# Starting the stages behind a row norm with one row tile at a time, in an eight-stage transformer kernel

## What is computed

```
x = first_block(x, ...)                       # ends: x + rms_norm(mixed @ w_o) * g
for layer in (0, 1):
    y = gla_mixer(x) if layer == 0 else moba_mixer(x)     # both end in @ w_out
    x = layer_norm_2(ALPHA * x + y, ln_g[layer, 0], ln_b[layer, 0])
    gate, up = split(x @ w_gu)                            # 1024 x 5632
    x = layer_norm_2(ALPHA * x + (silu(gate) * up) @ w_down, ln_g[layer, 1], ln_b[layer, 1])
# gla: q, k, v, g, gk_low = split(x @ w_in), chunked gated linear attention
# moba: q, k, v = split(x @ w_in), 8 heads of 128, q and k rotated (32 of 128 dims), softmax attention
```

## Time and profile before

| | |
|---|---|
| median of 3 runs | 929.03 us (928.59 to 933.44) |
| the profiled execution | 928.22 us |
| its span from first to last instruction | 926.5 us |
| PE busy | 888.3 us, 96% |
| DVE busy | 608.5 us, 66% |
| ACT busy | 438.6 us, 47% |
| POOL busy | 121.2 us, 13% |
| mean granted clock of PE | 0.986 |

### The profile page before, as it was taken

One profiled execution on the slowest core, in us unless ns is written; L12 is line 12 of the kernel. 1 busy time (PEld: TensorE's weight loads), 2 busy tenths in 40 slices (PEclk: granted clock), 3 DMA queues, 4 the chain that ended last, 5 costly groups with the idle time before them and its releaser, 6 DMA issues.

```text
span 926.5 us, 14261 instructions
## 1 busy us (share of the span) xinstructions
PE 888.3 (96%) x6011; PEld 813.1 (88%) x6011; DVE 608.5 (66%) x861; ACT 438.6 (47%) x606; POOL 121.2 (13%) x109
## 2 busy tenths in 40 slices
PE   6999989999999999989999999989999899999994
PEld 5997989998888888779999988779988899999883
DVE  5996995777567755784555544676887755555446
ACT  5555453555645853434444443334574444444330
POOL 0433430121002101020000000023600100000002
PEclk9999999999999999999999999989999999999998
DMA  8663665663347552546666555446634565655541
GB/s 300 190 181 91 190 189 143 175 170 112 104 127 237 170 162 81 167 144 189 187 186 182 183 186 192 151 153 195 192 114 141 172 187 184 183 182 185 192 146 46
DMA packets 117801, 154.20 MB, mean 166 GB/s; under 512 B 5263, under 2 KB 95786, under 8 KB 117706
## 3 DMA queue, kind: packets, MB, share of 16 engines
q1 hardware_dynamic: 116266, 148.31, 52.5%
q0 software_dynamic: 1472, 4.98, 1.7%
HBM read 151.44 MB, written 1.05 MB: 165 GB/s over the span
## 4 chain that ended last, share of the span: by engine, by line
PE 85%; DVE 12%; DMA 1%; issue 1%; ACT 1%; DVEq 0%; SPq 0%
PE acc L527 25%; PE acc L528 24%; PE acc L529 24%; PE acc L565 3%; DVE w_lo L1471 2%; DVE conv L1618 2%; DVE y L1902 1%; DVE rs L1504 1%; PE misc L653 1%; DVE stats L1889 1%; PE misc L717 1%; DVE y L1877 1%; DVE rs L1508 1%; DVE sc_acc L1638 1%; PE misc L898 1%
## 5 line engine op out<-in xcount | busy, mean ns | idle before, releaser
L1471 DVE TENSOR_TENSOR w_lo<-staged,w_hi 128x1024 fp32r<-128x1024 f32 x274 | 339.6, 1249 | 224.7 <-ACT w_hi L1073 224.2
L1073 ACT CAST w_hi<-staged 128x1024 fp32r<-128x1024 f32 x274 | 285.0, 1045 | 238.3 <-DMA staged<-in_ffn_w_gu 69.1
L527 PE MATMUL acc<-x_hi,w_hi 128*128 128x256 f32 (+1 forms) x1296 | 367.6, 284 | 3.1 <-DVE m L1697 3.1
L528 PE MATMUL acc<-x_lo,w_hi 128*128 128x256 f32 (+1 forms) x1296 | 366.9, 283 | 0.0
L529 PE MATMUL acc<-x_hi,w_lo 128*128 128x256 f32 (+1 forms) x1296 | 364.1, 281 | 0.0
L527 PEld LDWEIGHTS acc<-x_hi,w_hi 128*128 128x128 f32 x1296 | 243.7, 188 | 5.5 <-DVE m L1697 3.3
L529 PEld LDWEIGHTS acc<-x_hi,w_lo 128*128 128x128 f32 x1296 | 246.0, 190 | 0.0
L528 PEld LDWEIGHTS acc<-x_lo,w_hi 128*128 128x128 f32 x1296 | 244.4, 189 | 0.4 <-issue 0.2
L2258 POOL TENSOR_TENSOR y<-y,gain 128x512 f32<-128x512 f32 x8 | 10.7, 1338 | 460.1 <-ACT y L1269 460.1
L529 PE MATMUL acc<-w_hi,h_lo 128*128 128x512 f32 x176 | 69.6, 396 | 0.0
L527 PE MATMUL acc<-w_hi,h_hi 128*128 128x512 f32 x176 | 69.6, 395 | 0.0
(11 more groups left out here) (369 smaller groups left out, 1124.2 us busy)
## 6 DMA issues: line engine op xcount, KB each, us to landing
staged<-in_ffn_w_gu SPq DMA_DIRECT2D x88, 512.0 KB, 3.5
staged<-in_w_in SPq DMA_DIRECT2D x58, 512.0 KB, 3.7
staged<-in_ffn_w_down SPq DMA_DIRECT2D x44, 512.0 KB, 3.5
staged<-in_gla_w_in SPq DMA_DIRECT2D x24, 512.0 KB, 3.6
staged<-in_moba_w_in SPq DMA_DIRECT2D x24, 512.0 KB, 3.9
staged<-in_w_o SPq DMA_DIRECT2D x8, 512.0 KB, 3.7
staged<-in_gla_w_out SPq DMA_DIRECT2D x8, 512.0 KB, 3.6
staged<-in_moba_w_out SPq DMA_DIRECT2D x8, 512.0 KB, 3.6
```

The source lines that it names most:

```text
L527: pe.matmul(dst, st_hi, mv_hi, start=start, stop=False)
L528: pe.matmul(dst, st_hi, mv_lo, start=False, stop=False)
L1073: nc.scalar.copy(hi, raw).then_inc(rounded, 1)
L1471: nc.vector.tensor_tensor(lo, raw, hi, ALU.subtract).then_inc(split, 1)
```

## The change

The code is changed in these ways.

1. The stages behind a norm begin with a stage of 512 columns in row form, `n_first`: all of tile 0, then tile 1, with each group of transposes between its matmuls. For GLA it is the first half of v (`gla_v0`), for the FFN the first 512 gate columns, for MoBA the first half of v (`moba_v0`). The second halves of v follow q and k.
2. The gate columns of the FFN that are now in row form are copied to SBUF by ACT and turned back by PE, eight transposes in each layer, before the second up block.
3. The first group of transposes stands ahead of the last two k-slots' worth of tile 1's matmuls (six matmuls) in the stage before. `keep_awake` is gone from the boundaries.
4. Both tiles are normed on DVE, with two centring operations of 512 columns instead of four of 256. ACT's scaling and POOL's two operations for each half go.
5. DVE takes `rest_rows` of tile 0 and splits one more slot before it norms tile 1.
6. `down` ends by tile and half: (tile 0, half 0), (0, 1), (1, 0), (1, 1), twelve matmuls each.
7. MoBA's q and k come in alternating blocks of 256 columns. POOL rotates all of q and DVE all of k, one pair of heads at a time. The scores stand at positions 6, 7, 10, 11, 14, 15, 18, 19 of the 20 slots of q, k and the second half of v, each head's turned probabilities two positions later.

```diff
-STAGES += [("y_mla", 4), ("w_o", 8), ("gla_gk", 2), ("gla_q", 4), ("gla_k", 4), ("gla_v", 8), ("gla_g", 8),
-           ("gla_out", 8), ("gu0", 44), ("down0", 22), ("moba_q", 8), ("moba_k", 8), ("moba_v", 8), ("moba_out", 8),
+STAGES += [("y_mla", 4), ("w_o", 8), ("gla_v0", 4), ("gla_gk", 2), ("gla_q", 4), ("gla_k", 4), ("gla_v1", 4), ("gla_g", 8),
+           ("gla_out", 8), ("gu0", 44), ("down0", 22), ("moba_v0", 4), ("moba_qk", 16), ("moba_v1", 4), ("moba_out", 8),
...
-            def t_first(first, name, tag, count, halves=2):
-
-                turn_rows(tag, count)
+            def n_first(stage, name, tag):
+
                 open_out(name)
                 done = 4 * (int(tag[1]) - 1)
+                for t in range(TILES):
+                    rows = slice(t * P, t * P + P)
+                    if t == 1:
+                        turn_rows(tag, 2)
+                    for j in range(2):
+                        pe.wait_ge(s["x_rounded"], done + 2 * t + j + 1)
+                        for part in range(2):
+                            if part == 1:
+                                if j == 0:
+                                    turn_rows(tag, 2 * t + 1)
+                                await_read(pe, "%s_%d" % (tag, 2 * t + j))
+                            for q in (2 * j, 2 * j + 1):
+                                sl = Slot(FIRST[stage] + q, q)
+                                if t == 0 and part == 0:
+                                    ready(sl)
+                                for c in range(2):
+                                    k, cols = q * 2 + c, slice(c * 512, c * 512 + 512)
+                                    dst = acc[:, pair(name), t, :]
+                                    if part == 0:
+                                        pe.matmul(dst, xt_hi[:, k, rows], w_hi[:, sl.ring(), cols], start=k == 0, stop=False)
+                                        pe.matmul(dst, xt_hi[:, k, rows], w_lo[:, sl.ring(), cols], start=False, stop=False)
+                                    else:
+                                        mm = pe.matmul(dst, xt_lo[:, k, rows], w_hi[:, sl.ring(), cols], start=False,
+                                                       stop=k == KC - 1)
+                                if part == 1 and t == 1:
+                                    mm.then_inc(weights_used, 1)
...
+                        elif q == 3:
+                            turn_rows(tag, 0)
...
-                    if u == 0:
-                        keep_awake(b, 2)
-                        if count:
-
-                            pe.wait_ge(s["scaled0"], count - 1)
-                            keep_awake(b, 2)
-                            pe.wait_ge(s["scaled0"], count)
-                            keep_awake(b, 2)
-                    if u == 2:
-                        keep_awake(b, 2 if count else 5)
...
+                await_out(pe, "gate%d_rows" % layer)
+                for g in range(2):
+                    b = open_bank("gt%d_%d" % (layer, g))
+                    for c in range(2):
+                        for t in range(TILES):
+                            tr = pe.transpose(b[:, c * ROWS + t * P:c * ROWS + t * P + P],
+                                              gate_rows[:, t, (2 * g + c) * P:(2 * g + c) * P + P], ident)
+                    filled(tr, "gt%d_%d" % (layer, g))
...
+            for n in range(20):
+                if n < 16:
+                    name = "moba_%s%d" % ("qk"[n // 2 % 2], n // 4)
+                    if n % 2 == 0:
+                        open_out(name)
+                    t_slot(Slot(FIRST["moba_qk"] + n, n), pair(name), n % 2, xt_hi, xt_lo, first=n % 2 == 0, last=n % 2 == 1)
+                else:
+                    n_slots("moba_v1", ["moba_v1"], xt_hi, xt_lo, n - 16, n - 15)
+                heads_at(n)
+                if n in (16, 17):
+                    moba_pv(2 * n - 32)
+                    moba_pv(2 * n - 31)
...
+            def after_tail(stage, tag):
+
+                last = FIRST[stage] + COUNT[stage] - 1
+                round_rows(tag, 0)
+                round_rows(tag, 1)
+                lead(Slot(last - 1, 0))
+                round_rows(tag, 2)
+                round_rows(tag, 3)
+                lead(Slot(last, 0))
...
+                heads_at(n)
+                if n == 18:
                     moba_round(0)
                     moba_round(1)
...
+                if t == 0:
+                    rest_rows("x1", 0)
+                    rest_rows("x1", 1)
+                    lead(Slot(FIRST["w_o"] + 6, 6))
...
+                def centre(step):
+                    beside(step)
+                    if step < 2:
+                        cols = slice(step * 512, step * 512 + 512)
+                        nc.vector.scalar_tensor_tensor(y[:, t, cols], y[:, t, cols], mean, gain[:, cols], ALU.subtract, ALU.mult)
...
+                residual_moments(0, stage + "1", 1)
+                norm_tile(k, 0)
+                tag = "x%d" % (k + 2)
+                rest_rows(tag, 0)
+                slot_done(dve, stage, 7)
+                residual_moments(1, stage + "1", 1)
+                rest_rows(tag, 1)
+                lead(Slot(FIRST[stage] + 6, 6))
+                norm_tile(k, 1)
+                after_tail(stage, tag)
...
+            for j in range(4):
+                swap_halves("q", mq, mq_swap, j)
+                pool.wait_ge(s["swapped_q%d" % j], 32)
+                rotate(mq, mq_swap, r32, j, mrope_pool, trig[r32, 0, :], trig[r32, 1, :], s["mq_roped"], j + 1)
+                swap_halves("k", mk, mk_swap, j)
```

More of the change, by code:

```diff
@@ L312, in hybrid_stack @@
         hidden = place("hidden", [2, ROWS])
+        gate_rows = place("gate_rows", [TILES, 512])
         ffn_end = cursor[0]
@@ L1384, in swiglu @@
                     lead(sl)
-            def after_tail(k, stage, tag):
-                scale_tile0(k)
-                lead(Slot(FIRST[stage] + COUNT[stage] - 1, 0))
-                round_rows(tag)
-            after_tail(0, "gla_out", "x2")
-            swiglu(0)
-            after_tail(1, "down0", "x3")
-            for tag, dst in (("moba_q", mq), ("moba_k", mk)):
-                for sl in slots(FIRST[tag], 8):
-                    lead(sl)
-                    if sl.index % 2 == 1:
-                        slot_done(act, tag, sl.index)
-                        name = "%s%d" % (tag, sl.index // 2)
-                        copy_out(halves(dst, sl.index // 2), out_t(name), name)
+            after_tail("gla_out", "x2")
+            swiglu(0)
+            after_tail("down0", "x3")
+            for sl in slots(FIRST["moba_v0"], 4):
+                lead(sl)
+            rows_out(mv[:, :, 0:512], "moba_v0", "moba_v0")
             def moba_probsT(i):
@@ L1914, in norm_tile, with after_tail @@
                     nc.vector.scalar_tensor_tensor(x[:, t, cols], y[:, t, cols], r, shift[:, cols], ALU.mult,
-                                                   ALU.add).then_inc(s["x_ready1"], 1)
-                    if hf == 0 and k < 3:
-                        rest_rows("x%d" % (k + 2), [0])
-            rest_rows("x1", [2, 1, 3])
-            for stage in ("gla_gk", "gla_q"):
+                                                   ALU.add).then_inc(s["x_ready%d" % t], 1)
+            def after_tail(stage, tag):
+                rest_rows(tag, 2)
+                rest_rows(tag, 3)
+                lead(Slot(FIRST[stage] + COUNT[stage] - 1, 0))
+            after_tail("w_o", "x1")
+            for stage in ("gla_v0", "gla_gk", "gla_q"):
                 for sl in slots(FIRST[stage], COUNT[stage]):
@@ L1948, in _ @@
                                             ALU.subtract).then_inc(s["end_ready"], 1)
-            for sl in slots(FIRST["gla_v"], 8):
+            for sl in slots(FIRST["gla_v1"], 4):
                 lead(sl)
@@ L2071, in swiglu @@
                 norm_tile(2 * layer + 1, 0, tile1_half0)
+                if layer == 0:
+                    rest_rows("x3", 0)
                 slot_done(dve, stage, COUNT[stage] - 1)
                 residual_moments(1, names[1], 1)
+                if layer == 0:
+                    rest_rows("x3", 1)
+                    lead(Slot(FIRST[stage] + FCH - 2, FCH - 2))
                 norm_tile(2 * layer + 1, 1)
-            rest_rows("x2", [2, 1, 3])
-            lead(Slot(FIRST["gla_out"] + 7, 7))
@@ L2289, in _, with swap_halves @@
-            norm_tile0(3)
+            load_norm(1)
+            load_norm(2)
+            def swap_halves(name, src, swap, j):
+                hs = slice(2 * j, 2 * j + 2)
+                await_out(pool, "moba_%s%d" % (name, j))
+                for i in range(2):
+                    to, of = slice(i * ROPE // 2, (i + 1) * ROPE // 2), slice((1 - i) * ROPE // 2, (2 - i) * ROPE // 2)
+                    pool.dma_start(swap[to, hs, :], src[of, hs, :]).then_inc(s["swapped_%s%d" % (name, j)], 16)
```

340 lines of the change are left out of this document (151 added, 189 removed).

## The result

The changed kernel took 945.81 us (median of 4, 941.03 to 947.39) where the kernel before took 928.81 in the same comparison. The ratio on record, taken over all the runs, is 1.0172, interval 1.0149 to 1.0196 (that of the two medians is 1.0183). It is 1.7% slower, where the prediction said 927.3 us and at most 933.0.

What follows compares the result with a forecast made beforehand. PE, busy 96% of the span, bounds the kernel. Gains of 7.1, 0.3 and 0.5 less 1.8, 1.75 and 2.7 make 1.7 us: 928.22 to 926.5, or 927.3 us as a median; 8-in-10 range 920.5 to 933.0.

Steps and rivals of the forecast that it cites:

- boundaries at full clock: The four boundaries behind w_o, gla_out, down0 and moba_out: loss falls from 42.6 to 35.5 us, 7.1 gained.
- slow clock at them: Charge for slow clock at the four boundaries: 1.8 us, for one fall after down0's idle stretch of 4.6 us.
- MoBA: New PE waits for first scores, rounded heads and the copy of v: 2.7 us lost together, bounds 0 and 6.
- Boundaries, the new order: Step counting PE's waits at each boundary: losses of 9.1 (w_o), 8.0 (gla_out), 10.65 (down0) and 7.8 us (moba_out).
- I charge nothing for them and keep 1.8 each as the upper bound.: Boundary waits of 1.1 to 2.4 us, with transposes between: no clock fall charged, at most 1.8 us each.
- three boundaries: Sign that the prediction is wrong: the granted clock falls at three boundaries or more; it expected 0.50 only after down0.
- More slow clock: Rival: further clock falls at the four boundaries, 1.8 us each, up to 934.5 us with four; chance 0.18.
- nothing charged: GLA: q, k and v's 11 us less between k and the first product leave `ke` about 1 us early; no cost.
- (a): MoBA's first scores wait for pair 0 of q and k, swapped and rotated: 0.7 us, bounds 0 and 1.1.
- The others: MoBA's remaining waits: 0.2 us for rounding heads 0 to 3, 1.2 for v's copy, 0.6 for heads 4 and 5.
- DVE alone: Norms without POOL's multiply beside DVE: 0.5 us gained at the kernel's end, bounds -1 and 2; boundaries counted elsewhere.
- POOL and DVE exclude each other where it matters: Rival: in MoBA three later pairs of heads wait 0.7 to 1.5 us each: 929.4 to 931.8 us; chance 0.10.

Runs made afterwards that it cites:

- again: The changed kernel itself, unaltered, measured and profiled a second time: 942.05 us, ratio 1.0116 to the kernel before.
- trial 5: Changed kernel with filler matmuls put back into the boundary waits, half as many as in trial 1: 936.77 us, ratio 1.0084.
- trial 10: Kernel before with only tile 0's norm moved wholly to DVE behind gla_out, down0, moba_out and at the end, fillers kept: 923.67 us, ratio 0.9931.
- trial 1: Changed kernel with filler matmuls (`keep_awake`) put back into the waits of the four boundaries: 948.57 us, ratio 1.0241.
- trial 8: Kernel before without its filler matmuls at the four boundaries, nothing else: 931.84 us, ratio 1.0027.
- trial 6: Changed kernel with halved fillers, earlier fourth-slot split, earlier copy of V's first half and four earlier MoBA steps: 922.57 us, ratio 0.9935.
- trial 7: Kernel of trial 6 without its fillers: 928.55 us, ratio 1.0008 to the kernel before.
- trial 3: Changed kernel with ACT copying V's first half out of PSUM before waiting for that stage's last two slots: 938.51 us, ratio 1.0121.
- trial 4: Changed kernel with four MoBA steps earlier, among them the swap of the first k block: 936.67 us, ratio 1.0113.
- trial 11: Changed kernel with the halved fillers of trial 5 and the earlier MoBA steps of trial 4: 928.37 us, ratio 0.9984.
- trial 12: Kernel of trial 6 with the change at the w_o boundary undone: 918.01 us, ratio 0.9878 to the kernel before.

## Why the prediction was wrong

The terms of the sum, in us of the profiled execution's span, a minus for a gain:

| term | predicted | measured | again |
|---|---|---|---|
| boundaries at full clock | -7.1 | -6.3 | -6.3 |
| slow clock at them | +1.8 | +13.1 | +11.6 |
| gate transposes, row form | +1.4 | +1.4 | +1.4 |
| GLA | 0 | +4.1 | +2.5 |
| MoBA | +2.7 | +4.1 | +7.4 |
| end | -0.5 | -0.7 | -0.7 |
| start-up | 0 | +3.3 | -1.6 |
| sum | -1.7 | +19.0 | +14.3 |

The measured ones are differences of the table of stretches (MoBA's has 1.6 us of waits that lie at the head of moba_out's); their sums answer to spans 18.8 and 14.1 us longer. The row of slow clock is what trial 5 takes off the four boundary stretches. The boundaries as the prediction counts them lose 12.0, 11.0, 14.9 and 11.4 us in the changed kernel, 49.4 in all. Trial 5, with the same waits and no fall, is 13.1 under it: 36.3 against the 35.5 of the sum, and 42.6 before.

- **Boundaries, the new order: right.** Waits of 1.90, 1.01, 2.05 and 0.68 us stand at gla_out where 2.0, 1.1, 2.3 and 0.8 were predicted, 4.73 at down0 for 4.6. w_o's boundary gets worse, as the text said: it loses 9.4 us in trial 5 where 9.1 was predicted and 6.9 stood before.
- **The clock: the step that failed.** "I charge nothing for them and keep 1.8 each as the upper bound." The clock fell at all four boundaries, twice at two of them (the text had named three boundaries as what would make it wrong). One of these falls is the one charged, behind down0's 4.7 us. Each of the other five began within 2 us of the end of a wait of 1.9 to 2.3 us. The price was 2.6 to 3.9 us a boundary (trial 5 against the changed kernel), 11.6 to 13.1 in all, where 1.8 was charged. What was wrong is the condition. I took the length of a single wait, from before's 3.86, and shorter waits did it as well; but 2.7 us at gla_out in trial 10 and 3.4 us in MoBA in trial 1 were followed by no fall, so length alone doesn't decide. With the condition went the amount: 30.7 us of slow clock at the boundaries, where before has 13.7. The price of one us of it was about right: 13.1 / 30.7 = 0.43, where the text took 1.5 for 3 us and 2 for 6. It called those 6 us half filled; by the earlier trace rows PE was busy in 4.92 of them. And it missed the fall behind moba_out. The rival "More slow clock" had this mechanism, and even its far end, four falls, 934.5 us, priced it too low. The Trainium skill (TensorE: Matmul & The Clock Gate, Part 1), with slow as the default that recent activity releases, was the better guide: I had written that it speaks against taking `keep_awake` out, and then gave it no term.
- **`keep_awake` taken out: priced at nothing.** It costs 2.5 us in the old order (trial 8) and 6.8 in the new (trials 6 and 7).
- **GLA: "nothing charged" was wrong.** I had looked at `ke` and not at who empties the bank that q needs two stages later: ACT, behind two slots in its list. 1.9 us, with the clock up to 3.5 (trial 3).
- **MoBA: the right waits, too small a size.** (a), the wait for the first scores, was taken as 0.7 with an upper bound of 1.1; it was 1.6 to 6.7 in six executions, and 0 to 1.6 with k's swap issued earlier (trials 4, 6, 11). I took a swap as 3.4 us from issue to landing, as if that were fixed; among the weights' transfers it was 4.8 for k's first pair in trial 5, and between 2.3 and 5.1 over all the profiles. The others were 0.7 and 0.3 for mo_lo, where 0.2 and 0.6 were predicted, and 0.3 for the copy of v, where it was 1.2. The upper bound of 6 for the whole was passed in the second execution, in which the clock also fell behind the first scores.
- **DVE alone: right in direction, and the best part of the change.** I credited it with 0.5 at the end and left the rest inside the boundaries' sum. Alone it gives 6.4 us (trial 10). At the three boundaries behind a LayerNorm, with their stages, it gives 4.4 of the 9.6 us by which trial 12 is under before, and I didn't see it, since I never costed the part by itself.
- The rival "POOL and DVE exclude each other where it matters" held for the first pair in trial 5 alone; later pairs had the slack that I gave them.

Not settled: what decides whether a wait is followed by a fall. The same code at w_o is followed by one in some executions and not in others (43.15 and 45.65 us in stretches that differ only so), and a wait of 3.4 us for MoBA's first scores is in the second profile of the changed kernel and isn't in trial 1. How much of the 1.0172 against 1.0116 is this is not settled either.

## What to carry to other kernels

Price a slow clock by the work that lies under it, not by its length: a wait ahead of dense matmuls costs more than a longer one ahead of another wait, and an order that trades one long gap for four short ones in dense work can need fillers in them, sized from a measured filler. Cost every part of a change by itself, for the part that gains can hide in the sum of the one that loses. When a product is moved forward, follow its bank too: who empties it, and what stands ahead of that in the engine's list.

## What the runs showed of the hardware

- A filler of 256 columns in f32 is two matmuls in the trace, 0.45 us together, and a wait filled past its end costs the excess (3.3 us at gla_out in trial 1).
- The granted clock fell behind a single wait of 1.8 to 2.0 us between dense stretches in GLA in five of six executions, and not behind one of 1.2 us in a seventh.
- PE waits 3.1 us near 140 us in all fourteen profiles, always in the same code. Two show no fall behind it, and their start-up up to w_o takes 256.3 and 256.4 us. Ten show one of 3.4 us and take 257.6 to 258.0, and one shows 6.8 us and takes 259.2. So 3.4 us at 0.50 under dense matmuls cost 1.4 to 1.5 us. (The fourteenth is the first profile of the changed kernel with its slow beginning.)
- The two small transfers of a swap took 4.8 us from issue to landing (643.08 to 647.86 in trial 5) beside the weights' transfers, and 2.3 to 5.1 us over all the profiles.
